# One core, a two-layer decoder trunk: S5's token placement moved from ScalarE to GpSimd in layer 0, and the two late groups of own weights put into one column group

## The reference, cut to what matters

```python
xr = jnp.einsum('bsgc,gnc->bsgn', ug, bbr)          # ug: the input u in 32 groups of 16 channels
xi = jnp.einsum('bsgc,gnc->bsgn', ug, bbi)
...                                                  # h[s] = A * h[s-1] + x[s], A diagonal, complex
y = jnp.einsum('bsgn,gcn->bsgc', hr, c_re.astype(f32)) - jnp.einsum('bsgn,gcn->bsgc', hi, c_im.astype(f32))
y = y.reshape(B, S, W) + d_skip * uf
```

## Time and profile before

| | |
|---|---|
| median of 3 runs | 2420.36 us (2419.89 to 2423.72) |
| time of the profiled execution | 2422.44 us |
| its span in the profile | 2420.6 us |
| PE busy | 2345.2 us (97%) |
| DVE busy | 1861.5 us (77%) |
| ACT busy | 1303.4 us (54%) |
| POOL busy | 227.6 us (9%) |
| mean granted TensorE clock | 0.993 |

### The profile page before, as it was taken

One profiled execution on the slowest core, in us unless ns is written; L12 is line 12 of the kernel. 1 busy time (PEld: TensorE's weight loads), 2 busy tenths in 40 slices (PEclk: granted clock), 3 DMA queues, 4 the chain that ended last, 5 costly groups with the idle time before them and its releaser, 6 DMA issues.

```text
span 2420.6 us, 39998 instructions
## 1 busy us (share of the span) xinstructions
PE 2345.2 (97%) x13868; PEld 2051.6 (85%) x13868; DVE 1861.5 (77%) x2739; ACT 1303.4 (54%) x2202; POOL 227.6 (9%) x384
## 2 busy tenths in 40 slices
PE   6889999999999999999999999999999999999998
PEld 5679988788888888888889999887888888888887
DVE  7989998879999999666679987567895666565555
ACT  5376665545455545444468657655555445554444
POOL 1111111101111111000001130000110000000000
PEclk9999999999999999999999999999999999999999
DMA  9998888859999999787756865446795555555554
GB/s 379 404 381 315 297 282 312 307 192 359 339 342 344 337 347 338 246 291 269 278 209 220 299 242 197 165 179 266 286 335 190 187 190 190 186 188 203 197 193 145
DMA packets 189210, 643.04 MB, mean 266 GB/s; under 512 B 19089, under 2 KB 41809, under 8 KB 183329
## 3 DMA queue, kind: packets, MB, share of 16 engines
q1 hardware_dynamic: 125346, 421.72, 47.8%
q0 software_dynamic: 51264, 205.04, 23.7%
q10 hardware_dynamic: 12480, 14.72, 1.7%
HBM read 626.68 MB, written 14.71 MB: 265 GB/s over the span
## 4 chain that ended last, share of the span: by engine, by line
PE 78%; DVE 12%; DMA 4%; ACT 3%; issue 2%; POOL 0%; ACTq 0%; DVEq 0%; POOLq 0%; SPq 0%
PE ps L1307 25%; PE ps L805 18%; PE ps L1315 13%; PE ps L788 9%; PE ps L1204 4%; DVE w_lo L1966 3%; DVE ada_w L1972 2%; DVE mix L1966 2%; PE ps L773 2%; DMA ada_lo<-ada_d 1%; DMA ada_w<-ada_d 1%; PE ps L1218 1%; ACT w_hi L1388 1%; DVE side L1966 1%; DMA ring<-stream 1%
## 5 line engine op out<-in xcount | busy, mean ns | idle before, releaser
L1966 DVE TENSOR_TENSOR w_lo<-ring,w_hi 128x1024 fp32r<-128x1024 f32 x708 | 869.5, 1233 | 427.9 <-ACT w_hi L1388 423.7
L1388 ACT ACTIVATE w_hi<-ring 128x1024 fp32r<-128x1024 f32 x708 | 749.7, 1059 | 784.4 <-PE ps L805 244.8
L1307 PE MATMUL ps<-hT,w_hi 128*128 128x512 f32 x2688 | 642.2, 391 | 0.0
L1307 PEld LDWEIGHTS ps<-hT,w_hi 128*128 128x128 f32 x2688 | 493.9, 188 | 95.7
L1972 DVE SCALAR_TENSOR_TENSOR ada_w<-ada_w,cs_row 128x1024 f32<-128x1024 f32 (+1 forms) x332 | 406.7, 1259 | 15.6 <-DMA ada_w<-ada_d 15.2
L788 PE MATMUL ps<-hT,w_hi 128*128 128x256 f32 x2176 | 409.2, 290 | 8.7 <-DVE w_lo L1966 6.6
L788 PEld LDWEIGHTS ps<-hT,w_hi 128*128 128x128 f32 x2176 | 344.8, 195 | 19.1 <-issue 14.7
L1315 PEld LDWEIGHTS ps<-hT,w_lo 128*128 128x128 f32 x2688 | 344.6, 191 | 13.1
L1315 PE MATMUL ps<-hT,w_lo 128*128 128x256 f32 x2688 | 348.7, 283 | 0.0
L788 PE MATMUL ps<-hT,w_lo 128*128 128x256 f32 x1088 | 310.6, 286 | 0.0
L788 PEld LDWEIGHTS ps<-hT,w_lo 128*128 128x128 f32 x1088 | 211.5, 194 | 0.0
(11 more groups left out here) (323 smaller groups left out, 2357.8 us busy)
## 6 DMA issues: line engine op xcount, KB each, us to landing
ring<-stream SPq DMA_DIRECT2D x746, 512.0 KB, 4.7
ada_w<-ada_d POOLq DMA_DIRECT2D x320, 512.0 KB, 6.4
ada_w<-ada_d POOLq DMA_DIRECT2D x12, 1024.0 KB, 12.3
ada_lo<-ada_d POOLq DMA_DIRECT2D x10, 1024.0 KB, 15.8
ada_hi<-ada_d POOLq DMA_DIRECT2D x10, 1024.0 KB, 12.2
mix<-stream SPq DMA_DIRECT2D x14, 512.0 KB, 14.1
xs<-x SPq DMA_DIRECT2D x2, 2048.0 KB, 11.0
s_in_w<-mix ACTq DMA_DIRECT2D x8, 512.0 KB, 6.6
```

The lines of the kernel that those rows point to most:

```text
L1307: m = pe.matmul(ps[:, bank, :], w_hi[:, (c + half) % SPLIT, kk * P:(kk + 1) * P], hT[:, k, :, :], start=k == 0, stop=k == KT - 1)
L1388: s.activation(w_hi[:, c % SPLIT, :], ring[:, at % RING, :], ACT.Copy).then_inc(hi_ready, 1)
L1966: return v.tensor_tensor(o, a, b, op)
```

## The change

In layer 0, `s5_tokens` moves from ACT's list to GpSimd's. The 16 copies stand there in one run, behind the first four adaLN loads and ahead of all others, and the first waits until ACT has evacuated tile 3. Layer 1 keeps them on ACT. For the two late groups of own weights in layer 0, all four blocks go to PSUM partitions 0 to 31, block q at columns 128q and on, so they are in one column group; ACT's copy of a shift then takes all four blocks in one instruction of 32 partitions by 4 x 32(k + 1) elements. The products are issued block by block.

```diff
+        def own_rows(l, ut):
+            return l == 0 and ut >= len(HEAD_OWN)
+
+        def own_out(l, ut, q, n):
+            if own_rows(l, ut):
+                return ps[0:SC, 4, q * P:q * P + n]
+            return ps[SC * q:SC * (q + 1), 4 if l else 6, 0:n]
...
+                def s5_tokens(k):                                   # GpSimd
+                    if k == 0:
+                        in_ev.wait(pool, l, 4)
+                    for q in range(SQ):
+                        u = mix[SC * q:SC * (q + 1), T_U:T_U + 4, :].rearrange("p a (n s) -> p a n s", s=SL)
+                        m = pool.tensor_copy(s5_u2[SC * k:SC * (k + 1), q::SQ, :], u[:, :, :, SL - 1 - k])
+                    if k == SL - 1:
+                        s5_u.by(m)
+
                 ada_until(ASLOT)
                 for k in range(NT):
+                    if l == 0 and k < SL:
+                        s5_tokens(k)
...
-                    for part, name in ((0, "s_b_re"), (1, "s_b_im")):
+                    def product(part, q):
+                        name, j = ("s_b_re", "s_b_im")[part], SQ * ut + q
+                        pe.matmul(own_out(l, ut, q, P), A(name, SC * j, SC * j + SC),
+                                  pw_c[:, part, q, 0:SL, :].rearrange("p k c -> p (k c)"), start=part == 0, stop=False)
+                    def skip(q):
+                        qs = slice(SC * q, SC * q + SC)
+                        return pe.matmul(own_out(l, ut, q, SC), ident[:, qs], s5_skip(ut)[:, qs], start=False, stop=True)
+                    if own_rows(l, ut):
                         for q in range(SQ):
...
+                            product(0, q)
+                            product(1, q)
+                            m = skip(q)
...
                     for k in range(SL):
                         n = (k + 1) * SC
+                        to = pw_own[SC * k:SC * (k + 1), :, P - n:P]
+                        if own_rows(l, ut):
+                            m = s.activation(to, ps[0:SC, 4, :].rearrange("p (q x) -> p q x", q=SQ)[:, :, 0:n], ACT.Copy)
+                            continue
                         for q in range(SQ):
-                            m = s.activation(pw_own[SC * k:SC * (k + 1), q, P - n:P], ps[SC * q:SC * (q + 1), own_bank, 0:n], ACT.Copy)
+                            m = s.activation(to[:, q, :], own_out(l, ut, q, n), ACT.Copy)
...
-                        if n < HT + 4:
-                            s5_tokens(n - HT)                       # ACT, layer 0
```

More of the change, by code:

```diff
@@ L915, in s5_own_weights @@
                         in_ev.wait(pe, l, HT)
-                    for part, name in ((0, "s_b_re"), (1, "s_b_im")):
-                        for q in range(SQ):
[L918 to L923, removed]
+                    def product(part, q):
[6 more added lines that the diff above has]
+                    if own_rows(l, ut):
+                        for q in range(SQ):
+                            product(0, q)
+                            product(1, q)
+                            m = skip(q)
+                    else:
+                        for part in range(2):
+                            for q in range(SQ):
+                                product(part, q)
+                        for q in range(SQ):
+                            m = skip(q)
                     s5_own.by(m)
@@ L1641, in own_weights @@
                 def own_weights(ut):
-                    own_bank = 6 if l == 0 and ut < len(HEAD_OWN) else 4
                     s5_own.wait(s, l, ut + 1)
```

## The result

The changed kernel takes 2430.55 us (median of six runs, 2428.04 to 2433.15) against 2420.91 for the kernel before, a ratio of 1.0031 with a 95% interval of 1.002 to 1.0042. In a second set of twelve runs it took 2430.78 (ratio 1.0022, 1.0012 to 1.0033). It is slower. (The ratios come from the runs of one set and are not exactly the quotients of the medians, which would be 1.0040 and 1.0029.) The prediction said 2426 with a range of 2416 to 2433, its own forecast 2423.5 to 2430: the median lies in the range and just above the forecast's own. The profiled execution of the changed kernel took 2428.04 us, its span is 2426.3 against 2420.6: +5.7, where the prediction's sum says +5.9. It was the fastest of the six; the medians are 9.6 apart.

The account below looks back on a forecast made before the run. TensorE (PE busy 97%) was taken as the bound, closely following DVE between 140 and 270 us. DVE's +8.4, with +1.4, -2.4 and -1.5 on TensorE, gave +5.9 us: 2426 us, range 2416 to 2433.

Parts of the forecast that it names:

- its own forecast: Whole kernel: the summed time with its own range of 2423.5 to 2430 us, chance 0.45.
- What leaves ACT: ACT, layer 0: 10.7 us of placements and 4.8 us of own copies go; on the path only DVE's 1.08 and TensorE's L977 waits.
- What comes to PE: TensorE, late own-weight groups: 1.4 us more each (bounds 0 and 3.0), the first free before tile 14, the second paid.
- What comes to GpSimd: GpSimd, layer 0: 16 copies at 0.65 us each (bounds 0.33 and 1.3), 10.4 us if nothing holds them.
- What this does to DVE: DVE, from 150.7 us: turns taken with GpSimd cost 0.52 us a copy, 14 copies 7.3 us.
- What is queued behind the copies: GpSimd's next adaLN load: copies end near 172.6, load lands near 178.5, DVE waits 4.4 us, 2.2 more than before.
- The sum: DVE +8.4 us at tile 17; TensorE +8.4, +1.4 second group, -2.4 L977 wait, -1.5 clock: +5.9, nothing given back later.
- The prediction's last sentence: TensorE: the number would be wrong if longer idle times bring a low clock at tiles DVE does not hold back.
- (1): GpSimd copies beside DVE: cheap or not holding DVE, so not slower; -3.6 us, 2416.8, or +2.3; chance 0.27.
- (2): GpSimd copies: each costs 1.3 us because of the 16-byte read step; +13.3 us, 2433.7; chance 0.12.
- (3): Attention, later: TensorE's idle time there gives back 3 or 4 of the 5.9 us; +2, 2422.5; chance 0.12.
- (4): ACT's four own copies save nothing, ACT keeps 4.8 us; the L977 wait still goes, time as forecast; chance 0.04.

Follow-up runs that it names:

- writes without reads: Changed kernel with GpSimd's 16 copies replaced by 16 memsets of the same places, which read nothing: 2420.47 us, 0.9995 of the kernel before.
- own weights alone: Changed kernel with the placement copies put back on ACT, late own weights in one column group as changed: 2420.85 us, 0.9993 of the kernel before.
- the second profile: Profile of the changed kernel run once more, nothing altered: median 2430.78 us, ratio 1.0022, profiled span 2430.7.
- placement alone: Changed kernel with the own weights put back as before, only the placement copies on GpSimd: 2437.41 us, 1.0063 of the kernel before.
- the reordered version: Own weights in one column group, placement on ACT, `compress_sum`'s copy ahead of tile 17's own copies: 2420.68 and 2419.66 us, 0.9986 and 0.9989 of the kernel before.
- placement alone with `cmp_s` first: Placement on GpSimd, own weights as before, plus ACT making `compress_sum`'s copy ahead of the own copies at tile 17: 2432.78 us, 1.0035 of the kernel before.
- contiguous reads: Changed kernel with GpSimd's copies reading 256 neighbouring elements instead of every fourth: 2426.39 us, 1.0011 of the kernel before.
- late loads: Changed kernel with memsets for copies, GpSimd then waiting for ACT to evacuate tile 14 before the next adaLN loads: 2429.03 us, 1.0031 of the kernel before.

## Why the prediction came out as it did

**What leaves ACT**: right. The placements are worth nothing in time (writes without reads against own weights alone: 0.4 us apart). The own copies save 2 x 2.1 us, for 2 x 2.4. DVE's 1.08 before tile 16 was on the path, as the prediction said. For the second wait of `compress_sum` this isn't shown: it is gone in the changed kernel, but taking away this wait alone left the time at 2422.06 us (0.9996), so the 2.4 of the sum is no saving by itself.

**What comes to PE**: right, 2.2 us for a group against 0.7 (forecast 2.1), the first hidden before tile 14.

**What comes to GpSimd**: mis-sized. A copy takes 0.87 us where nothing holds it, between the 0.65 taken and the bound of 1.3. The contiguous copy took 0.40. The step of the reads, which the prediction put only into its upper bound, is worth a factor of two. The Trainium skill, page "GPSIMD Engine Reference", section "Performance pitfalls for Q7 kernels", has the direction right, with half as much again for such a step; these runs show about twice (0.87 and 0.40), and the estimate of 0.62 that the prediction made from the page is too low.

**What this does to DVE**: the mechanism is right, the size 7.3 is 5.1 (the last loaded chunk is done at 171.7 instead of 166.6): 15 instructions beside the copies take 21.1 us together instead of 15.1, and the idle 1.09 before 156.69 is gone. A copy longer than forecast took less from DVE than the forecast's shorter one was to take: 0.33 to 0.45 us against 0.52. The exclusion is one of reads, as the writes without reads show (0.83 instead of 1.16 for the same instruction). The Trainium skill, page "SBUF — State Buffer", section "Who interferes with whom", says just this, that a GpSimd instruction that only writes does not contend; the trace agrees, with 0.27 us for a memset and nothing for DVE.

**What is queued behind the copies**: right in time, partly by luck, and wrong in weight. The last copy was to end near 172.6 (172.26), the load to be there at 178.5 (178.57). The added wait is 4.5 where 2.2 was said, because DVE was done 2.3 us sooner. The sum of both is the forecast's to 0.1 us: 9.5 and 9.6. That the copies ended when forecast is luck in part: 172.6 was worked out as the end of some 14 DVE instructions (the fourteenth ended near 165.5 before, and DVE's 7.3 us come on top), and DVE lost 5.1. The fourteenth instruction beside the copies was done at 170.2; the copies ran beside fifteen, because DVE's idle time, in which two were to fit, was gone. The two errors, some 2 us each, cancel. And here the working of the prediction is at fault: it calls DVE's loss "the main term" and adds the load to it. The time of the next chunk is set by GpSimd's list (copies, issue, landing), and what DVE loses until then lies in its own wait. With DVE's loss taken away altogether and the loads as late, it came out at 2429.0. DVE matters for that list only through the taking of turns: 16 copies at 0.87 us would be done near 164.7 (an estimate), and they were done at 172.3.

**The sum**: up to tile 20 the steps came one by one. Tile 17 begins 7.7 us late (190.93, 198.61), DVE's `w_lo` for it 8.3 late (188.82, 197.07; forecast 8.4), tile 18 9.2 late (the second group), tile 19 6.5 (the wait of 2.4 is gone), tile 20 5.0 (the clock of 0.85 is gone). Forecast there was 5.9. Behind it the waits of 0.95 us at 230.15 and 1.45 at 262.87 make it 7.9 at tile 26, where the forecast was 5.9. That the spans then differ by 5.7 is luck: 4.1 of the 7.9 are gone by tile 28, because the kernel before has its slow spell there and this execution has none, and at 313.99 it is 6.5 late again. In the second profile the end is 10.1 us later than before. What the sum left out is the price of the 6.6 us wait in clock: tile 15 took 8.1 us (182.35 to 190.49) instead of 6.0 (172.98 to 178.93), but tile 17 was again there when its `w_lo` was. The 4.5 us between forecast and median are not in these steps. The profile they are read from is the fastest of six; the other profile has a load that is used 1.2 us later and the 1.4 us wait with a low clock behind it. The prediction's last sentence named this danger and gave it no price. The number came right within its range with these errors in it; what was right for the reasons given is that DVE loses time to the copies, that the load behind them is late, and that TensorE follows DVE.

**Rivals.** (1) falls, with its ground: one operand doesn't make a copy harmless. (2) is near on the copy beside DVE (1.35 us), not on the time. (3) is not what came: the second profile gives nothing back behind tile 26 (8.4 late there, 10.1 at the end), and in the first it is the missing slow spell that does. (4) falls in an instructive way. It says that without the saving in own copies the second wait goes all the same, "since TensorE is later". With placement alone TensorE is 8 us later and ACT too, the wait is 3.58, and the clock loss behind it some 5. The own weights are worth 1 to 2 us where ACT is ahead, and 6.9 (by the ratios 8 to 10) where it is not.

What is not settled: where, behind 240 us, the rest of the scatter between executions comes from, and whether the reordered version gains on own weights alone.

## What to carry to other kernels

Before work goes to an engine that seems idle, look at what stands behind it on that engine's list: here the copies stood ahead of loads that DVE needed, and putting them behind the loads gave back 4.3 of 9.7 us with the same instructions (by the ratios 1.5 to 3.6 of 7 to 9). Two delays that meet at one wait don't add up; ask which of them sets the time of the meeting, and take away each alone before saying which is the main term. And a wait of a few microseconds on TensorE can have a second price in the granted clock behind it, so edits that are each small can be far from additive.

## What the hardware showed that was not expected

- GpSimd, float32, 32 x 256, one input: 0.87 us (0.82 at least, in placement alone with `cmp_s` first) with reads at a step of 16 bytes, 0.40 with contiguous ones, 0.27 for a memset. Beside DVE the strided copy takes 1.35 in the median.
- DVE, two inputs in SBUF, beside such copies: +0.33 us (640 columns), +0.45 (1024) with the strided reads, +0.08 and +0.19 with the contiguous ones, 0 beside memsets. 15 DVE instructions ran beside 16 copies, a new one of each every 1.20 us where DVE's have 640 columns. GpSimd pays too: 16 copies took 21.55 us, where 16 x 0.87 would be 13.9.
- From the issue of the first of four adaLN loads in a run to DVE's use of it went 6.3, 7.5, 7.6 and 4.6 us in four executions of three kernels (the changed one twice, contiguous reads, late loads).
- In placement alone, TensorE's wait of 3.58 us lies at the start of 20 us with a granted clock of 0.79 and 0.70; 16 short matmuls took 3.67 us instead of 2.00 in them. The price is not fixed by the length of the wait: in the two profiles of the changed kernel the wait for `w_lo` before tile 13 is 3.09 and 3.10 us, and the stretch from 160 to 170 us has a granted clock of 0.82 in the first and 0.98 in the second (window, PE busy, clock, DMA share, GB/s):

```profile
160.00:170.00 10.00, 9.57 (x73) 0.82 0.51 177
```

```profile
160.00:170.00 10.00, 7.01 (x63) 0.98 0.54 188
```
